# Third block's mixer: slab units in quarters over eight scan steps, head-norm statistics in the loop, its tail by token halves

## What is computed

```python
u_l, v_l, q_l, k_l, vv_l, o_l, gt_l = split_proj(modulate(x, sh1, sc1) @ w_in[l])
hb_c, hb_l = mlstm_bidirectional(...)              # scan over 8 chunks of 128 tokens, both ways
y_a = spatial_gating(u, v, w_s, b_s, ln_v_g, ln_v_b)   # u * (w_s @ layer_norm(v) + b_s), by chunk
y_b = head_norm(h_b, hn_g) * jax.nn.sigmoid(o)         # layer norm of each head's 128 values
return jnp.concatenate([y_a, y_b], axis=-1) @ w_out
```

## Time and profile before

| | us |
|---|---|
| median of three runs (lowest, highest) | 3556.55 (3554.98, 3563.32) |
| the profiled execution, its own time | 3566.56 |
| its span | 3564.8 |
| PE busy | 3477.8 (98%) |
| DVE busy | 2526.7 (71%) |
| ACT busy | 1461.2 (41%) |
| POOL busy | 313.0 (9%) |

### The profile page before, as it was taken

How to read it: one execution, slowest core, us unless ns; L and a number is a source line. 1 busy time by engine, 2 the same in 40 slices (tenths; PEclk the granted TensorE clock), 3 DMA queues, 4 the chain that set the end, 5 groups by cost and what they waited for, 6 DMA issues and landing times. The chain is left out here.

```text
span 3564.8 us, 42922 instructions
## 1 busy us (share of the span) xinstructions
PE 3477.8 (98%) x16678; PEld 2830.7 (79%) x16678; DVE 2526.7 (71%) x3413; ACT 1461.2 (41%) x2057; POOL 313.0 (9%) x307
## 2 busy tenths in 40 slices
PE   9999999999999999999999999999999999999998
PEld 7977877888887788667777888876987768888887
DVE  5487588888877798453577876656547577888895
ACT  3345363333345422542443333335322266873123
POOL 0000012222222001230000000022000000000000
PEclk9999999999999999999999999999999999999999
DMA  3102111111112112111223232331131214667651
GB/s 133 48 1 98 45 42 54 54 54 54 54 60 95 54 51 69 37 64 56 89 65 107 98 101 98 115 115 60 55 72 51 83 47 154 241 249 294 241 203 60
DMA packets 112556, 331.25 MB, mean 93 GB/s; under 512 B 18349, under 2 KB 33325, under 8 KB 103778
## 3 DMA queue, kind: packets, MB, share of 16 engines
q1 hardware_dynamic: 112354, 328.51, 26.2%
HBM read 253.82 MB, written 66.13 MB: 90 GB/s over the span
## 5 line engine op out<-in xcount | busy, mean ns | idle before, releaser
L2836 DVE TENSOR_TENSOR residual<-residual,psum 128x512 f32<-128x512 f32 x224 | 149.5, 686 | 58.3 <-PE psum L2382 58.2
L2380 PE MATMUL psum<-parts_r 128*128 128x512 f32 x448 | 177.9, 397 | 3.9 <-DVE parts_r L2855 2.5
L2381 PE MATMUL psum<-parts_r 128*128 128x512 f32 x448 | 175.4, 391 | 0.0
L2382 PE MATMUL psum<-parts_r 128*128 128x512 f32 x448 | 175.3, 391 | 0.0
L3874 DVE SCALAR_TENSOR_TENSOR residual<-psum,ada,residual 128x512 f32<-128x512 f32 x192 | 137.6, 747 | 37.5 <-PE psum L3426 19.4
L1763 DVE TENSOR_TENSOR residual<-residual,psum 128x512 f32<-128x512 f32 x256 | 160.3, 687 | 0.0
L4269 DVE SCALAR_TENSOR_TENSOR mixer<-scratch,params,mixer 128x1024 f32<-128x1024 f32 x120 | 156.8, 1307 | 4.0
L1317 PE MATMUL psum<-mixer_r,parts_r 128*128 128x512 f32 x304 | 118.5, 390 | 0.7 <-ACT rows L1440 0.7
L1318 PE MATMUL psum<-gemm_input_r,parts_r 128*128 128x512 f32 x304 | 118.3, 389 | 0.0
L1319 PE MATMUL psum<-mixer_r,parts_r 128*128 128x512 f32 x304 | 118.3, 389 | 0.0
L3568 ACT ACTIVATE parts_r<-parts 128x1792 fp32r<-128x1792 f32 x24 | 41.0, 1707 | 180.3 <-DVE parts L3858 180.3
(11 more groups left out here) (949 smaller groups left out, 10839.2 us busy)
## 6 DMA issues: line engine op xcount, KB each, us to landing
y_blocks<-parts_r SPq DMA_DIRECT2D x84, 512.0 KB, 3.4
parts<-in_w SPq DMA_DIRECT2D x15, 1024.0 KB, 4.8
parts<-in_w_down SPq DMA_DIRECT2D x14, 1024.0 KB, 4.9
parts<-in_w_up SPq DMA_DIRECT2D x13, 1024.0 KB, 4.8
masks<-in_w_ada SPq DMA_DIRECT2D x48, 256.0 KB, 2.9
rows<-in_w_ada SPq DMA_DIRECT2D x48, 256.0 KB, 3.0
mixer_r<-y_blocks SPq DMA_DIRECT2D x12, 1024.0 KB, 9.5
low_r<-y_blocks SPq DMA_DIRECT2D x12, 1024.0 KB, 12.2
```

The costliest lines, as they stand in the source:

```text
L2380: pe.matmul(bank, w_high[:, kd, at], high[:, 2 * kd + n, :], start=start, stop=False, skip_group_check=True)
L2381: pe.matmul(bank, w_low[:, kd, at], high[:, 2 * kd + n, :], start=False, stop=False, skip_group_check=True)
L2382: return pe.matmul(bank, w_high[:, kd, at], low[:, 2 * kd + n, :], start=False, stop=stop, skip_group_check=True)
L2836: dve.tensor_tensor(x, x, ps, ALU.add).then_inc(drained, 1)
```

## The change

1. The slabs u0 and u1 are loaded, rounded and split by feature tile, as u0a, u0b, u1a, u1b. o2, o3 and u0a (six units) are cut into quarters of 2 x 3 matmuls; each of the steps 8 to 15 has three, one or two ahead of `intra` and the others behind `scores`. v1's pieces are now in steps 0, 1, 4, 5, the o1 units in 2, 3 and o0 in 6, 7. Behind the loop six units are left (`LATER`).
2. v is normalised with two operations per chunk, half of it in steps 5 and 6. The head statistics are taken by `bn_stats` per head and chunk in the loop (`stats_h`), combined behind it (`moments_h`), and applied in 32 operations of 128x128 (`normal_h`).
3. The bias of `spatial` is an fp32r product of 33 rows: ones times `b_s` rounded in row 0 and its low part in row 32, zeros between; POOL makes them.
4. Spatial units, transposes and gating go by token halves: groups 0, 2, 4, 6, then 1, 3, 5, 7. The rows of half 0 are rounded and split for the mix within this stage (`round_rows`, `low_rows`), and not in the next one.
5. X comes back in two halves, waited for in the next stage. The second load of mix weights is issued behind the last u1 unit. There are 8 constant products in place of 18 + 8 + 12.

```diff
--- before.py
+++ after.py
...
-    left_at = counted([(n, k) for n in range(2) for k in range(KT)])
+    left_at = counted([(1, k) for k in range(KT)])
...
-                return {k: (mix_lo, left_at[n, k]) for k in range(KT)}
+                return {k: (mix_lo, left_at[n, k]) for k in range(KT)} if n else {}
...
-            round_mix(0, range(0, 4))
             round_mix_pair(1)
-            round_mix(0, range(4, 8))
             round_mix_pair(2)
             round_mix_pair(3)
...
-            split_mix(0, range(0, 4))
             split_mix_pair(1)
-            split_mix(0, range(4, 8))
+            dve.wait_ge(c.x_landed[2], 32)
+            mix_drain(0, 0)
             split_mix_pair(2)
-            mix_drain(0, 0)
             split_mix_pair(3)
...
+    beside = {0: [("v1", 0), ("v1", 1)], 1: [("v1", 2), ("v1", 3)], 2: [("o1", 0, 0)], 3: [("o1", 0, 1)],
+              4: [("v1", 4), ("v1", 5)], 5: [("v1", 6), ("v1", 7)], 6: [("o0", 0, 0)], 7: [("o0", 0, 1)]}
+    spread_units = [("o2", 0, 0), ("o2", 0, 1), ("o3", 0, 0), ("o3", 0, 1), ("u0a", 0, 0), ("u0a", 0, 1)]
+    quarters = [(u, range(2 * q, 2 * q + 2)) for u in spread_units for q in range(4)]
+    before_intra, behind_scores, taken = {}, {}, 0
+    for j in range(8, 16):
+        for spot, count in ((before_intra, (1, 1, 2, 1)[j % 4]), (behind_scores, (2, 2, 1, 2)[j % 4])):
+            spot[j] = quarters[taken:taken + count]
+            taken += count
+    ended = lambda spot: [u for u, ks in spot if ks[-1] == KT - 1]
+    units += [u for j in range(8) for u in beside[j]] + spread_units
     SECOND = len(units)
-    units += [(w, m, n) for w in ("u0", "u1") for m in range(2) for n in range(2)]
+    LATER = [("u0b", 0, 0), ("u0b", 0, 1), ("u1a", 0, 0), ("u1b", 0, 0), ("u1a", 0, 1), ("u1b", 0, 1)]
+    units += LATER
...
+    GROUPS = (0, 2, 4, 6, 1, 3, 5, 7)
+    place = {g: i for i, g in enumerate(GROUPS)}
+    mixed_bank = lambda g: (2, 3, 4, 5, 3, 4, 5, 7)[place[g]]
+    turned_bank = lambda g: (7, 6, 0, 1, 6, 0, 1, 2)[place[g]]
...
-                if j == 9:
+                if j == 7:
                     sp.wait_ge(products, done_at["v1", 7])
                     load("o2")
                     load("o3")
+                if j == 12:
+                    sp.wait_ge(products, done_at["o2", 0, 1])
+                    load("u0a")
             sp.wait_ge(products, done_at["o3", 0, 1])
-            load("u0")
+            load("u0b")
+            sp.wait_ge(kw_ready, 18)
+            load("u1a")
             sp.wait_ge(acc_done, 16)
             sp.wait_ge(out_step, 16)
-            load("u1")
-            sp.wait_ge(products, done_at["u0", 1, 1])
+            load("u1b")
+            sp.wait_ge(products, done_at["u0b", 0, 1])
             if prefetch:
                 c.load_pair(sp, 0, c.PW[:, 4:8:2, :], prefetch, 0)
-            sp.wait_ge(products, done_at["u1", 1, 1])
-            sp.dma_start(c.X[:, :, :], c.spill).then_inc(x_back, 16)
+            sp.wait_ge(products, done_at["u1b", 0, 0])
+            sp.dma_start(c.X[:, :, halves[0]], c.spill[:, :, halves[0]]).then_inc(c.x_landed[2], 16)
+            sp.wait_ge(products, done_at["u1b", 0, 1])
             if prefetch:
                 c.load_pair(sp, 1, c.PW[:, 8:12:2, :], prefetch, 1)
-            sp.wait_ge(x_back, 16)
...
+            pool.wait_ge(tables_landed, 64)
+            pool.tensor_copy(ones_r, c.ones[0:BS_ROWS, :]).then_inc(pool_lo, 1)
+            for i in range(2):
+                pool.tensor_copy(bs_split[i], bs_in[:, 256 * i:256 * i + 256]).then_inc(pool_lo, 1)
+            pool.wait_ge(pool_lo, BS_READY - 2)
+            for i in range(2):
+                low = bs_split[i][32:33, :]
+                pool.tensor_tensor(low, bs_in[32:33, 256 * i:256 * i + 256], low.bitcast(F32), ALU.subtract).then_inc(pool_lo, 1)
 
         @block.tensor
...
-                if 4 <= j < 8:
-                    piece("v1", 2 * j - 8)
+                mine = beside.get(j, [])
+                if len(mine) == 2:
+                    piece(*mine[0])
+                for (w, m, n), ks in before_intra.get(j, []):
+                    unit(w, m, n, ks=ks)
                 intra(j)
                 if j < 15:
                     scores(j + 1)
-                if j < 4:
-                    unit(("o0", "o1")[j // 2], 0, j % 2)
-                elif j < 8:
-                    piece("v1", 2 * j - 7)
-                elif 9 <= j < 13:
-                    if j == 9:
-                        c.constant_products(pe, PS[:, 7, :], 18)
-                    unit(("o2", "o3")[(j - 9) // 2], 0, (j - 9) % 2)
+                if len(mine) == 2:
+                    piece(*mine[1])
+                elif mine:
+                    unit(*mine[0])
+                for (w, m, n), ks in behind_scores.get(j, []):
+                    unit(w, m, n, ks=ks)
...
+                bs = bs_split[g // 4][:, g // 2 % 2 * P:(g // 2 % 2 + 1) * P]
+                pe.matmul(out, ones_r, bs.unsqueeze(1).to_broadcast([BS_ROWS, 4, P]), start=True, stop=False, skip_group_check=True)
...
-            c.constant_products(pe, PS[:, 0, :], 8)
-            for m in range(2):
-                for n in range(2):
-                    unit("u0", m, n)
-            pe.wait_ge(tables_landed, 48)
-            pe.wait_ge(v_step, 24)
-            for g in range(4):
+            for u in LATER[:4]:
+                unit(*u)
+            pe.wait_ge(tables_landed, 64)
+            pe.wait_ge(pool_lo, BS_READY)
+            for g in GROUPS[:4]:
                 spatial(g)
-            for n in range(2):
-                unit("u1", 0, n)
-            transposes(range(0, 4))
-            for n in range(2):
-                unit("u1", 1, n)
-            transposes(range(4, 8))
-            for g in LAST:
+            transposes(GROUPS[:4])
+            pe.wait_ge(y_done, 1)
+            unit(*LATER[4])
+            for g in GROUPS[4:]:
                 spatial(g)
-            pe.wait_ge(written, 5)
-            c.constant_products(pe, PS[:, 2, :], 12)
+            transposes(GROUPS[4:])
+            pe.wait_ge(y_done, 5)
+            unit(*LATER[5])
+            pe.wait_ge(y_done, 6)
+            c.constant_products(pe, PS[:, 4, :], 8)
...
+            def round_rows(ks):
+                for k in ks:
+                    if k < 4:
+                        act.wait_ge(y_done, k + 1)
+                    else:
+                        act.wait_ge(written, k - 3)
+                    act.activation(c.MR[:, k, halves[0]], M[:, 4 + k, halves[0]], ACT.Copy).then_inc(rows_hi, 1)
...
+            round_slab("u1a")
             act.wait_ge(n_step, 6)
-            act.activation(var, var, ACT.Exp, scale=-0.5).then_inc(n_step, 1)
+            act.activation(head_rstd, head_rstd, ACT.Ln, bias=c.ln_eps[:, :]).then_inc(n_step, 1)
+            act.wait_ge(n_step, 7)
+            act.activation(head_rstd, head_rstd, ACT.Exp, scale=-0.5).then_inc(n_step, 1)
+            evacuate_u(LATER[0])
+            round_slab("u1b")
+            evacuate_u(LATER[1])
             act.activation(M[:, 8:12, :], M[:, 8:12, :], ACT.Sigmoid).then_inc(o_done, 1)
-            for n in range(2):
-                evacuate(("u1", 0, n), M[:, 6, halves[n]])
+            evacuate_u(LATER[2])
+            evacuate_u(LATER[3])
             if prefetch:
                 act.wait_ge(c.landed[0], base[0] + 16 * 7)
                 act.activation(c.PWR[:, 5, :], c.PW[:, 4, :], ACT.Copy).then_inc(split_hi, 1)
-            for n in range(2):
-                evacuate(("u1", 1, n), M[:, 7, halves[n]])
+            act.wait_ge(mixed, 4)
+            round_rows(range(0, 2))
+            round_rows(range(4, 8))
+            evacuate_u(LATER[4])
+            act.wait_ge(mixed, 8)
+            round_rows(range(2, 4))
+            evacuate_u(LATER[5])
...
+            def stats_h(j):
+                pos = H_PLACE[chunk[j]]
+                dve.wait_ge(out_step, j + 1)
+                for h in range(4):
+                    ins = dve.bn_stats(head_stats[:, pos, h, :], h_all[:, pos, h * P:(h + 1) * P])
+                ins.then_inc(h_added, 1)
+
...
+            def normal_h(n):
+                dve.wait_ge(n_step, 8)
+                for ch in range(4 * n, 4 * n + 4):
+                    for h in range(4):
+                        pos, g = H_PLACE[ch], 4 * H_PLACE[ch] + h
+                        x = h_all[:, pos, h * P:(h + 1) * P]
+                        ins = dve.tensor_scalar(x, x, head_mean[:, g:g + 1], head_rstd[:, g:g + 1], ALU.subtract, ALU.mult)
+                ins.then_inc(n_step, 1)
...
+            def low_rows(ks):
+                for k in ks:
+                    dve.wait_ge(rows_hi, rounded_at[k])
+                    dve.tensor_tensor(c.HR[:, k, halves[0]], M[:, 4 + k, halves[0]], c.MR[:, k, halves[0]].bitcast(F32), ALU.subtract)
...
+                if j >= 9:
+                    stats_h(j - 1)
                 if j < 13:
                     keys(5 + j)
-                if j == 9:
```

(92 more changed lines are left out.)

174 lines of the change are left out of this document (100 added, 74 removed).

## The result

| | before | the change |
|---|---|---|
| median of five runs (lowest, highest), us | 3557.51 (3554.98, 3563.32) | 3533.02 (3532.54, 3534.81) |
| profiled execution, own time / span | 3566.56 / 3564.8 | 3532.54 / 3530.8 |
| from step 8's `inter` to the first mix matmul | 133.18 | 107.99 |
| idle ahead of the first mix matmul, and again for a low row | 1.69, 0.64 | 0.30, 0 |

The ratio is 0.9925, 95% interval 0.9914 to 0.9937: 24.5 us faster, where 25.0 were forecast (3531.5). A further run of the kernel before, among those of e11, took 6050.84 us at a mean granted clock of 0.65 and is set aside.

A forecast was written before the change was run, and what follows sets the result against it. TensorE, busy 98% of the span, was taken as the bound; 9.1 + 10.6 + 2.1 - 0.35 + 1.7 + 1.8 = 25.0 us off the median 3556.55 gave 3531.5 us, range 3522 to 3544.

The forecast's parts named there:

- part 1: Loop steps 8 to 15: slab units in quarters, six in the loop instead of four, two fewer behind; gain 9.1 us.
- part 3: Spatial units: bias at 0.34 instead of 1.05 us, four units 5.7 us; gain 7.0 + 3.6 = 10.6 us.
- clock of the two units, lone start: Two units behind the first four spatial units: 2.1 us more if the clock stays up; one more lone unit start costs 0.35.
- constants at the end: Stage's end: 12 constant products took 3.63 us, 8 take 1.95; gain 1.7 us.
- waits at the boundary: First mix unit of the next stage: 2.3 us of waits for low rows shrink to 0.5; gain 1.8 us.
- 0.23 for each run that starts: Steps 8 to 15: each run of slab matmuls costs 0.23 us to start, 16 runs 3.7 us.
- a step that waits: Rival, steps 8 to 15: six units share one PSUM bank; one us lost in each of eight steps, 3539.5 us; 8%.
- Part 2: VectorE's head norm behind the loop: list ends some 17 us behind it, gating product wanted at 23; costed at 0.
- clock credit of 4.1 + 0.7 + 2.1: Spatial stretches and the two units behind the first: microseconds of the gain that come from the clock staying up.
- The rival of a falling clock: Spatial stretches: clock falls again, 6.2 us lost in one of two, 3537.7 us, or both, 3543.9; 14%.
- Part 4: Stage's end and next stage: fewer constants, 1.7 us, and low rows ready before the mix, 1.8 us.
- Under PE's work, so worth 0 by itself: Stage's end: SP's 13.0 us wait for X lies under TensorE's work, so no longer waiting for it gains 0.

The follow-up runs named there:

- e11: The kernel before, unchanged, run again for a second profile: median 3562.41 us, 133.09 us from step 8's inter to the first mix matmul.
- e2: The change with the six slab units whole, behind the scores in steps 8, 9, 10, 12, 13, 14, none ahead of intra: 3536.87 us, ratio 0.9936.
- e7: The change with each 128x128 head norm product cut into four of 128x32 (128 operations, not 32): 3542.30 us, ratio 0.9954.
- e5: The kernel before with only the new spatial bias (fp32r product of 33 rows, made by POOL): 3554.49 us, ratio 0.9986.
- e3: The change with the old spatial bias, an fp32 product with one row of contraction: 3546.39 us, ratio 0.9962; profiled execution 3542.33.
- e12: e5 with X brought back in two halves, both waited for in the next stage: 3551.86 us, ratio 0.9969.
- e9: e8 with SP's last two loads (second mix weights, half 1 of X) issued at the next stage's start: 3533.58 us, ratio 0.9916.
- e4: The change without the 8 constant products at the stage's end: 3538.26 us, ratio 0.9941.
- e8: The change with the first two later u units' banks traded, no constants, last u unit's copy and gating in the next stage: 3536.25 us, ratio 0.9935.

## Why the prediction was right

The forecast, 25.0 us, met 24.5. That it came within 0.5 is partly luck: the second pair of medians gives 27.0, and the terms read from the profiles add up to 25.8. By its own terms, from the profiles:

| term | forecast | read |
|---|---|---|
| part 1, two units fewer behind | 9.1 | 56.30 + 10.99 - 57.28 = 10.0 |
| part 3, spatial stretches | 10.6 | 12.73 + 9.30 - 5.97 - 5.96 = 10.1 |
| clock of the two units, lone start | 1.75 | 46.02 (8 units) - 33.20 (6) - 10.99 = 1.8 |
| transposes | 0 | 0.2 |
| constants at the end | 1.7 | 3.63 - 1.95 = 1.7 |
| waits at the boundary | 1.8 | 1.69 + 0.64 - 0.30 = 2.0 |
| sum | 25.0 | 25.8 |

**Part 1** was 0.9 short, of two errors against each other. "0.23 for each run that starts" is right behind `scores` (0.22) and wrong ahead of `intra` (0.02), 1.7 us in all; the 0.78 for the bank was left out. I had named the shared bank, but only for a step that waits, not for the loop's end. The argument that the quarters ahead of `intra` cover the scan's chain was right in its facts and empty in its worth: e2 does without them at the same time.

**Part 2** was right to cost the cover at 0. The list ended 18 us behind the loop (17 forecast), near the lower end of its bounds; the prediction had expected that a fixed latency for each instruction would bring it nearer the upper ones. The upper ends add up to 28.9 and not to 28, so against the bank wanted at 29 they left no room at all. The sizes were low where I went by length: 0.26 for a product (0.21), 0.87 for four statistics (0.8). e7 shows where 0 ends. I set the upper bound (0.54 for each) only against the first gating product; in e7, which goes beyond it (4 x 0.208 = 0.83), the first wait was for a low slab that stands in the middle of the list.

**Part 3** was 0.5 short in size, since the bias costs 0.43 and not 0.34. The clock credit of 4.1 + 0.7 + 2.1 was right in size, and partly by luck: the prediction named no cause for it. e5 and e11 show one: without the one-row fp32 products the clock stays up, with idle time, constants and order as they were. It isn't the only one, since in e3 the first stretch of the new order stays at 1.00 with the one-row products. The rival of a falling clock had its place (the second stretch, e3) but not its cause; with the short bias it appeared in none of the eleven profiles, in either order. The transposes of the change run at 1.00 and no run isolates them.

**Part 4** was right in sum. "Under PE's work, so worth 0 by itself" is right for X before, but by 0.7 us only, and misleading: part 3's second 3.3 us hang on it (e5, e12), and the 1.7 us of constants, which also stood behind X's issue, should hang on it too, which no run tests alone. Of these 1.7, 0.8 is clock and not constants: in e5 the same twelve took 2.84 at 1.00, and 3.63 before. I counted the constants as gain; e9 shows that what they covered, SP's two issues, was a further 1.6 to be had, and e4 that taking them out alone can cost 1.7.

Not settled: what it is in the old bias that lets the clock fall (the new one has more rows, another number format and less than half the length, and no run changes one of these alone); why it falls in the second stretch in e3 and in the first one before; and where the 4 us between e3's profiled execution and its median lie.

## What to carry to other kernels

A transfer or a list that is hidden is hidden by certain work: when the same change shortens that work, cost the cover again, before giving the gain away (e5 lost 3.2 of 12 us to the wait, and 2.0 to the clock behind it). At a stage boundary look at every engine that has something left, and the queue that issues loads first, since it shows up as busy nowhere. Where the scatter of the runs is larger than the term, read the term in a stretch between two fixed instructions; it repeated here to 0.1 us where the medians of one kernel moved by 2 to 5.

## What the runs showed of the hardware

A matmul with one row of contraction (fp32, 512 columns) takes 1.05 us from start to start, and spatial units with it brought the granted clock from 2.4 to 1.2 GHz for part of the time (0.63 over 12.7 us before, 0.89 over 9.3 in e3), though not in the first such stretch of e3; with 33 rows in fp32r, at 0.43 us, those stretches stayed at 2.4 in every profile. A VectorE product of 128x32 costs 0.208 us and one of 128x128 0.261. The two loads ahead of the boundary took 0.55 and 0.61 us of SP's time to issue (e8), and the boundary waits for that. After 1.9 us of idling without constants the clock fell for 3.4 us in one profile (e4) and stayed in another (e8); after 4.93 us of idling it fell for 4 us (e5).
